# Turning the second head of a biased pair right behind the first

## The reference, cut to what matters

```python
for l in range(DEPTH_2):                      # two layers
    h = rmsnorm(x, norm_mix[l])
    proj = jnp.einsum('bsd,de->bse', h, w_in[l])
    qa, ka, va, qb, kb, vb, qc, kc, vc = jnp.split(proj, IN_SPLITS_2, axis=-1)
    oa = window_attention(qa, ka, va, a_sink[l], t5_table)        # branch A: bias, mask, sink
    ob = neighborhood_attention(qb, kb, vb, b_rpb[l])             # branch B: bias, mask
    oc = axial_global_attention(qc, kc, vc, c_q_gain[l], c_k_gain[l])   # branch C: no bias
    mix = jnp.concatenate([rmsnorm(oa, out_gain_a[l]),
                           rmsnorm(ob, out_gain_b[l]),
                           rmsnorm(oc, out_gain_c[l])], axis=-1)
    x = x + jnp.einsum('bse,ed->bsd', mix, w_o[l])
    h = rmsnorm(x, norm_mlp[l])
    u = jax.nn.relu(jnp.einsum('bsd,df->bsf', h, w_up[l]))
    x = x + jnp.einsum('bsf,fd->bsd', u * u, w_down[l])
```

## Time and profile before

| What | before |
|---|---|
| median of three runs | 3290.59 us |
| the profiled execution, its own time | 3293.72 us |
| its span, first to last instruction | 3291.5 us |
| PE busy | 3269.2 us (99%) |
| DVE busy | 2173.1 us (66%) |
| ACT busy | 1621.8 us (49%) |
| POOL busy | 921.1 us (28%) |
| mean granted clock of PE | 0.997 of full speed |

### The profile page before, as it was taken

One profiled execution on the slowest core, in us unless ns is written; L12 is line 12 of the kernel. 1 busy time (PEld: TensorE's weight loads), 2 busy tenths in 40 slices (PEclk: granted clock), 3 DMA queues, 4 the chain that ended last, 5 costly groups with the idle time before them and its releaser, 6 DMA issues.

```text
span 3291.5 us, 48452 instructions
## 1 busy us (share of the span) xinstructions
PE 3269.2 (99%) x19126; PEld 2862.2 (87%) x19126; DVE 2173.1 (66%) x3072; ACT 1621.8 (49%) x2697; POOL 921.1 (28%) x821
## 2 busy tenths in 40 slices
PE   9999999999999999999999999999999999999998
PEld 8989888888888897788888888889788888888887
DVE  6668687754676668778764477555778775457654
ACT  5457464443444545555443344444655544344443
POOL 2434132210232224255220033112336331013221
PEclk9999999999999999999999999999999999999999
DMA  7654546755566554555656566555365556555554
GB/s 262 194 170 142 178 156 215 229 189 195 185 192 192 186 186 128 172 153 187 192 190 194 184 189 190 193 192 179 123 177 170 187 190 193 191 187 190 189 194 143
DMA packets 188280, 604.57 MB, mean 184 GB/s; under 512 B 36597, under 2 KB 41573, under 8 KB 188054
## 3 DMA queue, kind: packets, MB, share of 16 engines
q1 hardware_dynamic: 188054, 601.47, 57.3%
HBM read 599.16 MB, written 8.00 MB: 184 GB/s over the span
## 4 chain that ended last, share of the span: by engine, by line
PE 88%; DVE 5%; ACT 3%; issue 1%; POOL 1%; DMA 1%; SPq 0%; DVEq 0%; POOLq 0%; ACTq 0%
PE ps L1879 87%; DVE wl L2508 3%; ACT wh L2238 1%; ACT sS L2334 1%; PE ps L1882 1%; DVE sS L2512 1%; POOL acc L2872 0%; DVE xr L2508 0%; DVE den L2652 0%; DMA xr<-in_x 0%; DVE x L2516 0%; DMA wt<-in_w_in 0%; DMA wt<-in_w_vsl 0%; ACT tA L2238 0%; DMA sS<-rpm 0%
## 5 line engine op out<-in xcount | busy, mean ns | idle before, releaser
L2508 DVE TENSOR_TENSOR wl<-wt,wh 128x1024 fp32r<-128x1024 f32 (+3 forms) x1108 | 1466.0, 1355 | 303.1 <-ACT wh L2238 286.9
L1879 PE MATMUL ps<-x,wh 128*128 128x512 f32 x4448 | 1562.0, 393 | 3.0 <-DVE wl L2508 2.2
L1879 PE MATMUL ps<-x,wl 128*128 128x256 f32 x4448 | 1254.7, 282 | 0.0
L2238 ACT ACTIVATE wh<-wt 128x1024 fp32r<-128x1024 f32 (+3 forms) x1108 | 1118.0, 1048 | 270.0 <-PE ps L1879 235.7
L1879 PEld LDWEIGHTS ps<-x,wh 128*128 128x128 f32 x4448 | 836.4, 188 | 183.3 <-issue 4.9
L1879 PEld LDWEIGHTS ps<-x,wl 128*128 128x128 f32 x4448 | 841.8, 189 | 0.6
L1879 PE MATMUL ps<-ua,wh 128*128 128x512 f32 (+1 forms) x2432 | 832.5, 386 | 0.0
L1879 PE MATMUL ps<-ua,wl 128*128 128x256 f32 x2368 | 667.8, 282 | 0.0
L2508 DVE TENSOR_TENSOR tB<-ps,tA 128x256 f32<-128x256 f32 x422 | 177.2, 423 | 726.8 <-ACT tA L2238 726.2
L2238 ACT ACTIVATE tA<-ps 128x256 f32<-128x256 f32 x422 | 158.8, 380 | 944.4 <-PE ps L1879 944.2
L1879 PE MATMUL ps<-ub,wh 128*128 128x512 f32 x1536 | 536.6, 390 | 0.0
(11 more groups left out here) (236 smaller groups left out, 1865.5 us busy)
## 6 DMA issues: line engine op xcount, KB each, us to landing
wt<-in_w_up SPq DMA_DIRECT2D x384, 512.0 KB, 4.4
wt<-in_w_down SPq DMA_DIRECT2D x384, 512.0 KB, 4.8
wt<-in_w_in SPq DMA_DIRECT2D x156, 512.0 KB, 4.6
wt<-in_w_o SPq DMA_DIRECT2D x64, 512.0 KB, 4.6
wt<-in_w_out SPq DMA_DIRECT2D x32, 512.0 KB, 3.9
wt<-in_w_vb SPq DMA_DIRECT2D x16, 512.0 KB, 4.2
wt<-in_w_va SPq DMA_DIRECT2D x16, 384.0 KB, 3.6
wt<-in_w_vsl SPq DMA_DIRECT2D x8, 512.0 KB, 7.2
```

Of the source, the lines that this page charges most:

```text
L1879: return eng.matmul(o, l, r, start=start, stop=stop, skip_group_check=True)
L2238: return eng.activation(o, i, ACT.Copy, **kw)
L2508: return eng.tensor_tensor(o, a, b, op)
```

## The change

In `two_heads` the second head's turn was put into `late`, which runs at n = 13 of the same unit. Now, for a pair with bias, as long as the norm of branch C of the layer has not begun, it is called right behind the first head's turn, at n = 8. In all other cases it stays late.

```diff
@@ -1299,7 +1299,10 @@
             yield
         pts = [sP.grab() for _ in hds]
         turn_head(hds[0], pts[0], 0)
-        late.append(lambda: turn_head(hds[1], pts[1], 1))
+        if bias and (hds[1][0], "C") not in branch_norms:
+            turn_head(hds[1], pts[1], 1)
+        else:
+            late.append(lambda: turn_head(hds[1], pts[1], 1))
         yield
         while not has("a_v", *v):
             yield
```

## The result

The changed kernel takes 3297.20 us (median of 13 runs, 3291.32 to 3299.25), the kernel before in the same comparison 3288.79 us (13 runs, 3287.85 to 3291.36). The ratio is 1.0022, with a 95% interval of 1.0014 to 1.0029. So it is slower by 8.4 us, just over the 0.2% that can be told from no change. The forecast was 3295.5 us, its range 3288 to 3303 us.

The account below looks back on a forecast made before the run. PE, busy 99% of the span, was taken as the bound. Gains, new waits and half clock summed to +0.35 us in the first layer and +4.5 in the second, +4.9 on the 3290.59 us median: 3295.5 us, range 3288 to 3303.

Parts of the forecast that it names:

- The turns themselves: All 12 moved turns on PE, 6 a layer, together cost 0, with bounds of 0.6 us in all.
- The copy of the second head: Branch A's products with v no longer wait for DVE's copy: 0.99 us go in the first layer, 1.33 in the second.
- The 0.3 us a layer: Part of the copies' gain given back because PE arrives sooner at weights DVE prepares; chosen between 0 and 0.65 us.
- The norm of branch C: First layer only: 2.86 us of PE's wait for POOL's power and 1.65 us of half clock go, 4.5 us together.
- The wait at B2's scores: PE waits 3.9 us in each layer for kb2, now behind B3's masks on POOL; bounds 2.1 to 7.0 us.
- The clock: Half clock on PE behind each new wait costs 1.65 us, between 0 and 3.3 us.
- The key projections: kb0 and kb1 also stand behind their own pairs' masks; the forecast held them covered with mean stretches, not the longest.
- The rival that had waits elsewhere: Slower, by kb0 and kb1 behind their masks too; priced with 5.5 us waits at B2: +9.8 us, 3300.4 us; chance 0.33.

Follow-up runs that it names:

- e1: Changed kernel, but the second score buffer is let go only at n = 13, so bias, masks and scores keep the units of before; 3294.51 us.
- e5: The kernel before, unchanged, run once more for a second trace; 3290.13 us.
- e7: Changed kernel with the early turn in the first layer only; 3293.78 us.
- e2: Changed kernel with only the pairs of branch A turned early; 3286.84 us.
- e6: Changed kernel with POOL's mask additions one unit behind the bias transfers, so B3's come behind kb2; 3289.79 us.
- e9: Changed kernel with A3's division by the sums put at n = 13, behind B0's row maxima on DVE; 3293.16 us.
- e11: The changed kernel, unchanged, run once more for a second trace; 3297.63 us.
- e4: Changed kernel with the scores of B1 and B2 held back one unit, until the next pair's projection qb is there; 3284.59 us.

## Why the prediction was right, and where it was not

The time was in the range and the main mechanism is the one forecast, but that it is only 1.7 us off is luck. The forecast was a change of +4.9 us, measured are +8.4; its base, a median of three, lay 1.8 us above the later one; and the terms of the sum are off by up to 4.5 us either way. By its steps:

**The turns themselves, 0: right.** A group of eight at 1368.67 is followed by the next scores at 1369.63, 0.96 us; before it was 0.52 us for the first head and 0.44 us for the lone one, 0.96 us together.

**The copy of the second head: right, a little small.** All products with v last 1.09 us. Against the second trace of before (1.73 and 1.76 us in the first layer; 1.60, 1.17 and 1.90 in the second) 1.3 and 1.4 us go. One reading was wrong: the 0.9 us that the earlier trace rows have for `sP` are two products with v of branch C (1284.84 and 2343.98), and they are still there after the change; the wait of branch A shows only in the length of its groups. The 0.3 us a layer that I gave back at the weights is not there: `wl` has 2.7 us in five places before and after. e1 shows where such a gain is given back instead: at the norm, where POOL's queue is last.

**The norm of branch C, -4.5 us: the wait went as forecast, but most runs do not seem to have had it.** This is the step that failed in size. The sum was made against one profiled execution that lay 4.6 us above the later median of before (3289.1 us), and 3.5 us of that excess are this one wait and its half clock (e5). One detail of the reading is off too: between the last mask and the power only one operation is slow (`accs`, 1.71 us; kb3 takes 0.75), and the power itself is the other.

**The wait at B2's scores, 3.9 us a layer: right, and 1 us too large.** Measured 2.97 and 3.05 us, in the second trace 2.11 and 3.21, in e7 3.60. The chain was SP's issue, landing, masks, kb2, as written; landing and masks took 9.1 us instead of 10.06. e2 and e6 show the masks to be the cause.

**The clock, 1.65 us behind each new wait: right in the first layer, half of it in the second,** where 3.4 us are lost in both traces.

**The key projections.** The forecast left B1 without a wait; that is wrong. The rival that had waits elsewhere, 0.33, named B1 but by the masks. In fact kb1's masks were long done, and ACT and DVE were late (e9); the masks matter only by slowing DVE (e11). It needed a look at which other score moved next to its own projection. Its time, 3300.4 us, is 3.2 us off, the forecast's 1.7 us.

**Summed anew**, layer by layer: the first from the start of A0's product with v to the same point of the second layer, the second from there to the end of the span. All against the second trace of before (1035.2 and 876.6 us).

| trace | first layer, us | second layer, us |
|---|---|---|
| e4, no new wait | -2.2 | -2.4 |
| changed, waits and their half clock | +4.3 and +1.7 | +4.3 and +3.4 |
| changed, sum of both rows, and measured | +3.8, +3.7 | +5.3, +5.2 |
| e11, waits and their half clock | +2.1 and +1.7 | +4.6 and +3.4 |
| e11, sum with e4's row, and measured | +1.6, +1.5 | +5.6, +5.5 |

So the waits, the clock behind them and e4's gain account for both traces of the changed kernel. In the forecast's terms: +4.9 as forecast, +4.5 for the norm's wait that was not there to be gained, -1.8 for B2, +2.6 for B1, +1.8 for the clock, and -2.9 for a gain of 4.6 us in place of 1.7 make +9.1 us; the two layers of the first trace have +8.9 us, the medians differ by 8.4.

The half clock that only the second trace of before has, ahead of the change, cost nothing. PE in the first trace, and then a window and PE's timeline in the second:

```profile
1284.84 1.08 PE L1879 MATMUL ps<-sP,vc 128*64 128x256 f32 x4 [0.52 <-DVE sP L2827]
1285.85 0.66 PE L1882 MATMUL ps<-idt,sS 128*128 128x128 f32 x4
```

```profile
1277.00:1281.00 4.00, 4.00 (x16) 3.53 (x17) 3.57 (x7) 1.77 (x3) 0.90 (x2) 0.57 0.24 39
1285.90 0.66 PE L1882 MATMUL ps<-idt,sS 128*128 128x128 f32 x4
```

At 1281 PE was 1.3 us behind the first trace, but the next product with v of branch C waits for its copy in any case, and behind it the difference is 0.05 us. Half the length at 1.2 GHz is what it costs only where PE finds no wait afterwards that takes it up.

What stays open: why e4 gains 4.6 us when the copies explain 2.7 us. The clock is not the reason: from A0's product with v to 3270 us the mean is 1.00 in both traces, and over all runs of that comparison before and e4 have the same mean clock, 0.998. About 0.5 us a layer stand in four couples behind the norm (1484.51 to 1486.40 in the second trace of before, 1.89 us where four take 1.39). The rest was not found. Nor was it settled why the half clock lasts twice as long in the second layer.

## What to carry to other kernels

A step that frees buffers a little earlier moves whole steps by a unit, so list for each consumer how far it now stands behind its producer on every engine, not only behind the one whose queue you had in mind. Before you count on the removal of a wait, take a second profile: a profiled run some microseconds above the median may, as here, hold a wait that most others don't have. And where scores moved up and their keys did not, moving them back one unit (e4) kept the gain and had none of the waits. And an engine's operations can be late because of another engine that it never waits for (POOL's masks and DVE's divisions, e11).

## What the runs showed of the hardware that I had not expected

- Waits of 2.0 to 3.6 us on PE were followed by 3.4 us at 1.2 GHz in some cases (2.01 us in e9's second layer), by none in another (2.00 us in e6) and by 6.9 us in others (3.05 and 3.21 us). Length of the wait alone does not tell; none of 1.43 us or less had any in these stretches. At 1277 us the clock fell in two traces (e5, e7) behind a group of scores of branch C that lasted 2.13 us instead of 1.14, a wait of 1.0 us inside it; in the first trace of before the same group, as long, had no half clock behind it.
- The same POOL addition of 128 x 256 takes 0.73 us alone and 1.7 us beside DVE's split of weights, and a power of 128 x 2 numbers 0.71 and 1.69 us: such a small one pays the same extra microsecond. It looks like a wait and not like a lower rate, which is an inference.
- The collision goes the other way too: beside four mask additions DVE's pair of splits took 3.07 us instead of 2.36 (e6), and A3's divisions 4.0 us instead of 2.3 (e11).
- 3.4 us at 1.2 GHz cost 1.3 us of PE's time at 1281 us and 0.05 us at 1286 us, because a wait that was there anyway took them up.
